# Where the weights, activations and inner rows begin in SBUF: from the 128-byte grid to 16 bytes past it

## What is computed

```python
def first_block(x, ...):
    h = x
    for i in range(2):                       # 0: gated DeltaNet, 1: MoBA attention
        hn = rmsnorm(h, mix_norm_g[i])
        h = h + mixer_i(hn)                  # hn @ w_in, the mixer, @ w_out
        h = h + square(relu(rmsnorm(h, mlp_norm_g[i]) @ w_up[i])) @ w_down[i]   # 1024 -> 4096 -> 1024
    return rmsnorm(h, final_norm_g)

def second_block(x, mem, ...):
    h = rms_norm(x)
    branches = diff_attention, forgetting_attention, conv_branch, short_conv    # all from h @ w_in
    mixed = sum(sigmoid(h @ w_gate) * (branch_n @ w_branch[n])) @ w_out
    x = x + rms_norm(mixed)
    x = x + rms_norm(cross_attention(rms_norm(x), mem) @ w_xo)
    return x + rms_norm((silu(u_g) * u_v) @ w_down)     # u = conv over tokens of rms_norm(x) @ w_up
```

## Time and profile before

| | |
|---|---|
| time, median of 3 runs | 1251.89 us (1251.63 to 1254.33) |
| the profiled execution: span from the first to the last instruction | 1249.1 us |
| its own time | not recorded apart from the span |
| TensorE matmuls busy | 1220.7 us, 98% |
| weight loads busy | 1106.9 us, 89% |
| VectorE busy | 871.6 us, 70% |
| ScalarE busy | 700.5 us, 56% |
| GpSimd busy | 56.3 us, 5% |
| transferred | 210.80 MB, mean 169 GB/s |

### The profile page before, as it was taken

How to read it: one execution, slowest core, us unless ns; L and a number is a source line. 1 busy time by engine, 2 the same in 40 slices (tenths; PEclk the granted TensorE clock), 3 DMA queues, 4 the chain that set the end, 5 groups by cost and what they waited for, 6 DMA issues and landing times.

```text
span 1249.1 us, 21521 instructions
## 1 busy us (share of the span) xinstructions
PE 1220.7 (98%) x8583; PEld 1106.9 (89%) x8583; DVE 871.6 (70%) x1252; ACT 700.5 (56%) x1016; POOL 56.3 (5%) x102
## 2 busy tenths in 40 slices
PE   8999989999999999999999999999999999999997
PEld 7999988888888998888888999999999977888886
DVE  5888567666666656666656589998656577778876
ACT  4984555555455554554554564656454456666663
POOL 5010020000000001000000000000000010000000
PEclk9999999999999999999999999999999999999999
DMA  7671134666554654565555565354546534555561
GB/s 223 197 203 68 38 122 150 222 214 202 186 184 151 203 165 141 166 211 180 184 185 167 172 210 184 118 162 145 179 150 203 186 107 147 174 194 190 201 201 68
DMA packets 160340, 210.80 MB, mean 169 GB/s; under 512 B 5542, under 2 KB 143220, under 8 KB 160261
## 3 DMA queue, kind: packets, MB, share of 16 engines
q1 hardware_dynamic: 157315, 202.77, 50.6%
q0 software_dynamic: 1904, 6.85, 1.4%
q10 hardware_dynamic: 1042, 0.07, 0.1%
HBM read 208.62 MB, written 1.05 MB: 168 GB/s over the span
## 4 chain that ended last, share of the span: by engine, by line
PE 79%; DVE 10%; ACT 4%; issue 2%; DMA 2%; SPq 1%; POOL 1%; DVEq 0%; POOLq 0%; ACTq 0%
PE bank L369 16%; PE bank L373 16%; PE bank L372 16%; PE bank L454 15%; PE bank L450 8%; DVE wlo L305 3%; ACT whi L297 2%; PE bank L1425 2%; DMA raw<-in_dn_w_in 1%; DVE common L2582 1%; PE bank L2003 1%; PE bank L1445 1%; ACT common L753 1%; SPq L3388 1%; PE bank L2095 1%
## 5 line engine op out<-in xcount | busy, mean ns | idle before, releaser
L305 DVE TENSOR_TENSOR wlo<-raw,whi 128x2048 fp32r<-128x2048 f32 x190 | 434.9, 2291 | 203.6 <-ACT whi L297 203.3
L297 ACT ACTIVATE whi<-raw 128x2048 fp32r<-128x2048 f32 x190 | 363.3, 1913 | 145.4 <-PE bank L369 43.5
L369 PE MATMUL bank<-xparts,whi 128*128 128x256 f32 x912 | 262.5, 288 | 0.4 <-DVE common L2764 0.4
L373 PE MATMUL bank<-xparts,wlo 128*128 128x256 f32 x912 | 258.7, 284 | 0.0
L372 PE MATMUL bank<-xparts,whi 128*128 128x256 f32 x912 | 258.6, 284 | 0.0
L454 PE MATMUL bank<-xparts,whi 128*128 128x512 f32 x832 | 208.0, 392 | 0.0
L369 PEld LDWEIGHTS bank<-xparts,whi 128*128 128x128 f32 x912 | 175.5, 192 | 2.8 <-issue 2.1
L372 PEld LDWEIGHTS bank<-xparts,whi 128*128 128x128 f32 x912 | 175.6, 192 | 0.6 <-issue 0.5
L373 PEld LDWEIGHTS bank<-xparts,wlo 128*128 128x128 f32 x912 | 175.5, 192 | 0.0
L454 PEld LDWEIGHTS bank<-xparts,whi 128*128 128x128 f32 x832 | 149.8, 189 | 26.9
L369 PE MATMUL bank<-whi,hhi 128*128 128x512 f32 x392 | 153.1, 391 | 3.8 <-DVE hlo L1061 2.3
(11 more groups left out here) (391 smaller groups left out, 1706.2 us busy)
## 6 DMA issues: line engine op xcount, KB each, us to landing
raw<-in_mlp_w_up SPq DMA_DIRECT2D x32, 1024.0 KB, 5.5
raw<-in_mlp_w_down SPq DMA_DIRECT2D x32, 1024.0 KB, 5.1
raw<-in_w_in SPq DMA_DIRECT2D x22, 1024.0 KB, 5.3
raw<-in_w_up SPq DMA_DIRECT2D x22, 1024.0 KB, 5.2
raw<-in_w_gate SPq DMA_DIRECT2D x16, 1024.0 KB, 5.5
raw<-in_dn_w_in SPq DMA_DIRECT2D x15, 1024.0 KB, 5.8
raw<-in_mb_w_in SPq DMA_DIRECT2D x12, 1024.0 KB, 5.2
raw<-in_w_down SPq DMA_DIRECT2D x11, 1024.0 KB, 4.9
```

The lines of the kernel that those rows point to most:

```text
L297: nc.scalar.activation(whi[:, s, :], raw[:, r, :], ACT.Copy).then_inc(hi_ready, 1)
L305: nc.vector.tensor_tensor(wlo[:, s, :], raw[:, V % RAW, :], f32(whi[:, s, :]), ALU.subtract).then_inc(lo_ready, 1)
L369: ins = pe.matmul(o, shi, mhi, start=first, stop=False, skip_group_check=True)
L373: return pe.matmul(o, slo, mhi, start=False, stop=last, skip_group_check=True)
```

## The change

The five tensors `whi`, `wlo`, `xparts`, `hhi` and `hlo` are each allocated 32 floats (128 bytes) larger, and the kernel uses the part that begins 4 floats (16 bytes) in. All views that are made of them (`xhi`, `xlo`, `smh`, `sml`, the gate rows) move along. Since each grows by 128 bytes, every tensor behind them keeps its place modulo 128: `bhi` and `blo` are 32 bytes past a multiple of 128 before and after. `raw` keeps its address. No instruction is added, removed or moved.

```diff
         raw = sb("raw", [P, RAW, UNIT])
-        whi = sb("whi", [P, RING, UNIT], F32R)
-        wlo = sb("wlo", [P, RING, UNIT], F32R)
-        xparts = sb("xparts", [P, 2, KT, T], F32R)
+        PAD, W_AT, X_AT, H_AT = 32, (4, 4), 4, (4, 4)
+        whi, wlo = (sb(n_, [P, RING * UNIT + 32], F32R)[:, at_:at_ + RING * UNIT]
+                    .rearrange("p (s n) -> p s n", s=RING) for n_, at_ in zip(("whi", "wlo"), W_AT))
+        xparts = sb("xparts", [P, 2 * KT * T + PAD], F32R)[:, X_AT:X_AT + 2 * KT * T]\
+            .rearrange("p (x k t) -> p x k t", x=2, k=KT)
         xhi, xlo = xparts[:, 0], xparts[:, 1]
-        hhi = sb("hhi", [P, 2, 2, T], F32R)
-        hlo = sb("hlo", [P, 2, 2, T], F32R)
+        hhi, hlo = (sb(n_, [P, 4 * T + 32], F32R)[:, at_:at_ + 4 * T]
+                    .rearrange("p (a b t) -> p a b t", a=2, b=2) for n_, at_ in zip(("hhi", "hlo"), H_AT))
```

## The result

| | before | after |
|---|---|---|
| median of 17 runs each, us | 1252.02 (1249.59 to 1254.73) | 1256.66 (1253.67 to 1258.30) |
| ratio, 95% interval | | 1.0030 (1.0023 to 1.0037) |
| span of the profiled execution, us | 1249.1 | 1252.7 (its own time 1254.39) |

By the ratio, the changed kernel is slower by 0.3%, 3.8 us (the two medians lie 4.6 us apart; the ratio is used throughout). That is little, but more than the 2.5 us that the prediction called no change.

What follows compares the result with a forecast made beforehand. TensorE was taken as the bound, busy in 98% of 1249.1 us. Terms 0 + 0.2 + 0 + 0 gave a span of 1249.3 us; with the runs' median 2.8 us above the profile's span, 1252 us, range 1239 to 1270.

Steps and rivals of the forecast that it cites:

- Step 1: 6296 TensorE matmuls with both operands moved: operands stay 0 apart on the 128-byte grid, pitches unchanged, 0 us.
- The other reading in step 1: Same 6296 matmuls priced like rows 32 bytes past: -9.8, +7.8 and +2.8 us, together +0.8, on the chain +0.7.
- The ratio on the chain: Five TensorE matmul lines: about 890 us of chain over 1050 us of pitches, so pitch changes count 0.85 in time.
- Step 2: 720 matmuls with bhi or blo: distance goes from 32 to 16 bytes, +0.2 us; 32 with row_parts taken as 0.
- Step 3: VectorE and ScalarE accesses to the moved tensors (L305, L297, L1061, L1050): odd starts cost nothing, 0 us.
- Step 4: The padding of the allocations: no instruction or transfer added, raw keeps its address, 0 us.
- The distance counts over more than 128 bytes: New operand distances of 128, 256, 384 bytes change pitches, either sign; one third of slower's 0.34, half of faster's 0.28.
- Off the grid costs: Moved matmuls' operand reads need one more 32-byte piece each side: +9 us, 1261 us; two thirds of slower's 0.34.
- The lock at 120 breaks: 256-column matmuls leave their settled 120.0 ns, 512-column ones keep theirs: -8.3 us, 1244 us; half of faster's 0.28.

Runs made afterwards that it cites:

- the shift alone: Against the kernel before: all five tensors in one allocation, no padding between, starting 16 bytes past the grid, distances as before; 1252.59 us, ratio 1.0014.
- The fastest kernel: Against the kernel before, unshifted: modulo 256 bytes xparts stands 192 further on than the weights, hhi and hlo 0; 1241.63 us, ratio 0.9914.
- the gaps alone: Against the kernel before: each of the five tensors grows by 128 bytes as in the change, but none is shifted; 1252.39 us, ratio 1.0012.
- the kernel at 64 past: Against the kernel before: the change's 128-byte paddings, but all five tensors begin 64 bytes past the grid instead of 16; 1254.27 us, ratio 1.0030.

## Why the prediction was right or wrong

The forecast was 1252.0 us, no change. It came to 1256.66, inside the range, by the ratio 3.8 us slower, just past the bound of "no change". That it came so near is in large part luck. By the prediction's own sign ("wrong if the pitches change by more than 0.5 ns on average") its mechanism is wrong: every kind with both operands moved left its pitch, by 1.6 to 6.3 ns, and only with the signs kept is the mean about 0.5 ns.

**Step 1 failed**: "their operands stay 0 apart on the grid of 128 bytes ... 0 us". It rested on two assumptions, and the runs refute both. The grid is not of 128 bytes: 128 apart moves every pitch, 256 apart none. In the changed kernel whi and xparts are 256 apart, but wlo and xparts, and whi and hhi, are 128 apart modulo 256. And "nothing in a common shift changes how the two reads stand to each other" is wrong for 16 bytes: the shift alone gives 118.1 and 231.0 for 119.7 and 226.9. The rows of before could not show either, since the five tensors hold no pair 128 apart and none of them begins off a multiple of 32.

**The other reading in step 1 met the numbers, by luck.** The prices at 32 past, worked out there for "being off the grid", were -2.3, +6.4 and +3.4 ns for the three shapes; measured were -1.6, +6.3 and +2.9. That reading said that gain and loss nearly cancel (+0.8 us), and they did (+3.2 us by the pitches of these kinds). But its rows do not show a start off the grid: bhi and blo stand 32 bytes from the weights, which is a distance, and a common start 32 past changed no pitch.

**The ratio on the chain was one number where it needed two.** Fitted over the 13 kernels (after and the twelve experiments; two unknowns by least squares, no kernel off by more than 1.5 us), a us of change in the 256-column pitches is worth 0.61 us of time and one in the 512-column pitches 0.77; the prediction had 0.85 for both. The fastest kernel's page shows where the rest goes: its pitches sum to -17.7 us, its time fell by 10.8, and TensorE's share of the chain fell from 79% to 70%, that of VectorE rose from 10 to 14% and of ScalarE from 4 to 7%. About 60% of the 512-column matmuls lie in the two MLPs of the earlier trace rows, where TensorE is never idle; many of the 256-column ones lie in the mixing stage, which VectorE nearly fills. That this is why the two differ is argued, not shown. For the change it means -6.5 x 0.61 + 9.3 x 0.77 = +3.2 us, with 3.8 measured.

**Step 2** was small, as priced, but had the sign wrong: 576 x +0.4 and 144 x -5.2 ns, -0.5 us where +0.2 was taken. Both are inside its bounds (the 144 went from 233.4 to 228.2). Its distance "from 32 to 16" holds modulo 128 alone: the five paddings add up to 640 bytes, so modulo 256 bhi and blo stand 144 bytes from whi and 16 from wlo afterwards.

**Step 3** was right: L307 took 2289 ns and L299 1913, where 2291 and 1913 were named. These two instructions of VectorE and ScalarE show no price of the start.

**Step 4** was right for what it priced, instructions and transfers, and missed that padding also sets distances: with nothing shifted it costs 0.12%.

**The rivals.** "The distance counts over more than 128 bytes" named one half of the cause. Its test, that xparts with whi and xparts with wlo part, came out (116.8 and 119.6 ns), but does not show it: the pair that moved is the one that is 256 apart, which its distance alone, modulo 256, would have left where it was, and neither the gaps alone (119.1 and 119.3) nor the shift alone (118.1 and 117.9) parts them. Nor do the two "differ in nothing else": they differ in their place in the stream, and had 119.9 and 119.4 before. The half is shown by the experiments with gaps and not by this test. "Off the grid costs" had the sign, but not its mechanism: its 32-byte pieces would have made every line slower, 121 to 123 ns and 229 or more, and the 256-column lines got quicker. Its price rested on an excess over the columns of 13.3 ns for both shapes; by its own rows that is 13.3 and 13.7 before, and after the change it is 11.4 and 19.9, so it does not go with the weight load alone. The rival was right in so far as 16 past differs from 0 while 32 and 64 don't. "The lock at 120 breaks" had the 256 columns right in the mean (xparts with wlo kept its pitch), and failed because the 512-column ones did not keep theirs.

**The rules.** The Trainium skill, SBUF — State Buffer, section "Door 1: The DMA port swizzle", gives 16-byte lines; in these runs a common shift by 16 bytes changes TensorE's pitches and one by 32 or 64 doesn't, so 16 bytes are not a whole step here. The Trainium skill, SBUF — State Buffer, section "Who interferes with whom", has PE's two read ports independent; the same instructions at other distances took 114.6 to 119.7 ns, which that rule would not let one expect.

**What stays open.** The runs show that distance and start set the pitches, and how much; they don't show by what mechanism. Why 192 is the best for activations and 0 for inner rows, and why 160 and 224 are not between their neighbours, is open. So is how the price goes by single pairs. With the gaps alone, xparts with whi, 256 apart, did not keep its 119.9 ns (119.1), and at 128 apart one and the same pair took mostly anything from 115 to 122 ns from one matmul to the next. In the kernels with all five gaps whi and wlo also stand 128 bytes from each other, and no run separates that from their distances to the activations. Part of the 0.3% of the kernel at 64 past is open too.

## What to carry to other kernels

In this kernel, where TensorE is the bound and each matmul loads its own weights, the placing of the moving against the stationary operand is a tuning knob of its own: 0.9% by 512 bytes of padding a partition, with no instruction changed. It had to be set apart for activations and for inner rows, modulo 256 bytes, and measured, because it isn't smooth; a padding that is added for alignment turns that knob too. Read it from the start-to-start distances on the timeline, for each shape and each pair of tensors, and look in each stage whether TensorE is the bound before multiplying by the count. And when a forecast of "no change" nearly comes true, look whether its terms stayed at 0 or cancelled: here 6.5 us of gain hid most of 9.3 us of loss.

## What the runs showed of the hardware that was not expected

- A matmul in fp32r of 256 columns with its own weight load and activations moving took 114.4 to 119.7 ns from start to start, one of 512 columns with inner rows 226.9 to 233.3 ns, at a granted clock of 2.4 GHz, by how far apart the operands stand (0 and 256 bytes alike, 64, 128 and 192 not) and by their common start (0, 32 and 64 alike, 16 not).
- The two shapes differ in which distance suits them: of those tried with nothing shifted, 0 is the best for the 512 columns (226.9) and the worst for the 256 columns (119.7), whose best is 192 (114.7).
- A gap of 256 bytes between the operands gives the time of no gap (ratio 1.0000, 0.9991 to 1.0010); its profile shows a mean granted clock of 0.946 and the pitches of before all the same, which is not explained.
